# Moving the rounding of finished q and k slabs to the end of their slot in a two-layer hybrid encoder kernel

## The reference

```
h = rmsnorm(x, g_mix[l]);  proj = h @ w_in[l];  q, k, v of groups A, B, C = split(proj)
A: a = softmax(q0 k0' - slope*dist) - lam * softmax(q1 k1' - slope*dist);  o = rmsnorm(a @ v, g_sub) * (1 - lam_init)
B: p = softmax with sink over the window of 128 back;  o = p @ v
C: s = q k' + cum_q - cum_k, causal;  o = softmax(s) @ v
x = x + concat(o_a, o_b, o_c) @ w_out[l]
x = x + square(relu(rmsnorm(x, g_mlp[l]) @ w_up[l])) @ w_down[l]
```

## Time and profile before

| | |
|---|---|
| time, median of 3 runs | 2723.97 us (2723.39 to 2725.60) |
| the profiled execution: time and span | 2725.2 us and 2723.4 us |
| PE busy / weight loads busy | 2586.7 us (95%) / 2121.5 us (78%) |
| DVE, ACT, POOL busy | 1156.1 us, 897.2 us, 214.7 us |
| mean granted PE clock | 0.978 |
| attention stretch of layer 0, about 80 to 607 us | PE busy 476.9 of 527 us |
| MLP of layer 0, 607 to 1372 us | PE busy 762.2 of 765 us |

### The profile page before, as it was taken

One profiled execution on the slowest core, in us unless ns is written; L12 is line 12 of the kernel. 1 busy time (PEld: TensorE's weight loads), 2 busy tenths in 40 slices (PEclk: granted clock), 3 DMA queues, 4 the chain that ended last, 5 costly groups with the idle time before them and its releaser, 6 DMA issues.

```text
span 2723.4 us, 33992 instructions
## 1 busy us (share of the span) xinstructions
PE 2586.7 (95%) x12825; PEld 2121.5 (78%) x12825; DVE 1156.1 (42%) x2309; ACT 897.2 (33%) x1572; POOL 214.7 (8%) x101
## 2 busy tenths in 40 slices
PE   7999999879999999999999999997899999999998
PEld 6778777668788888888878877776788888888886
DVE  5554566644322323223336546665533232232333
ACT  5554444432311202112236444444322021120222
POOL 1111011012000000000211111111110000000011
PEclk9999999989999999999999999998999999999998
DMA  5100010211111111111320000002111111111112
GB/s 170 60 24 24 16 31 25 63 45 39 46 54 46 46 54 44 49 46 54 100 79 24 24 24 24 24 24 68 47 47 46 54 45 48 46 54 46 46 46 77
DMA packets 219021, 131.44 MB, mean 48 GB/s; under 512 B 15222, under 2 KB 214432, under 8 KB 218664
## 3 DMA queue, kind: packets, MB, share of 16 engines
q1 hardware_dynamic: 213208, 114.38, 14.6%
q10 hardware_dynamic: 5712, 15.73, 1.5%
HBM read 117.47 MB, written 12.62 MB: 48 GB/s over the span
## 4 chain that ended last, share of the span: by engine, by line
PE 80%; DVE 7%; ACT 5%; issue 5%; DVEq 1%; DMA 0%; POOL 0%; SPq 0%; ACTq 0%; POOLq 0%
PE ps L1139 70%; PE ps L1271 2%; PE ps L1218 2%; PE ps L1291 2%; ACT probs L638 1%; DVE probs L945 1%; DVE probs L917 1%; ACT pt_hi L656 1%; PE ps L1293 1%; DVEq L924 1%; ACT sink_exp L641 1%; DVE pt_lo L968 1%; ACT o_out L673 0%; DVE wide_lo L963 0%; ACT wide_hi L651 0%
## 5 line engine op out<-in xcount | busy, mean ns | idle before, releaser
L1139 PE MATMUL ps<-wide_hi,w_hi 128*128 128x512 f32 x3016 | 962.1, 400 | 49.3 <-POOL w_lo L510 12.2
L1139 PE MATMUL ps<-wide_lo,w_hi 128*128 128x512 f32 x3016 | 939.8, 393 | 0.0
L1139 PE MATMUL ps<-wide_hi,w_lo 128*128 128x512 f32 x3016 | 937.0, 392 | 0.0
L1139 PEld LDWEIGHTS ps<-wide_hi,w_hi 128*128 128x128 f32 x3016 | 554.7, 190 | 183.8 <-issue 56.7
L1139 PEld LDWEIGHTS ps<-wide_lo,w_hi 128*128 128x128 f32 x3016 | 572.5, 190 | 122.9
L1139 PEld LDWEIGHTS ps<-wide_hi,w_lo 128*128 128x128 f32 x3016 | 571.5, 189 | 122.6
L719 ACT ACTIVATE w_hi<-w_raw 128x1024 fp32r<-128x1024 f32 x112 | 117.8, 1052 | 453.1 <-PE ps L1139 443.6
L638 ACT ACTIVATE probs<-probs,neg_max,slope 128x256 f32<-128x256 f32 (+7 forms) x256 | 202.4, 791 | 178.2 <-DVE neg_max L932 115.2
L723 ACT ACTIVATE ring<-ring 128x1024 f32<-128x1024 f32 x64 | 67.8, 1060 | 487.7 <-DVE ring L1074 487.7
L1094 DVE TENSOR_TENSOR xt<-ps,xt 128x1024 f32 x48 | 58.8, 1224 | 387.3 <-PE ps L1139 387.3
L968 DVE TENSOR_TENSOR pt_lo<-ps,pt_hi 128x512 fp32r<-128x512 f32 (+3 forms) x216 | 126.4, 585 | 221.7 <-ACT pt_hi L656 221.0
(11 more groups left out here) (139 smaller groups left out, 1842.8 us busy)
## 6 DMA issues: line engine op xcount, KB each, us to landing
w_raw<-in_w_up_dram SPq DMA_DIRECT2D x128, 256.0 KB, 3.0
w_raw<-in_w_down_dram SPq DMA_DIRECT2D x128, 256.0 KB, 3.0
w_raw<-in_w_in_dram SPq DMA_DIRECT2D x92, 256.0 KB, 3.3
x_saved<-xt ACTq DMA_DIRECT2D x16, 512.0 KB, 2.6
w_raw<-in_w_out_dram SPq DMA_DIRECT2D x32, 256.0 KB, 3.3
xt<-x_saved SPq DMA_DIRECT2D x16, 512.0 KB, 4.0
o_out<-cum_saved ACTq DMA_DIRECT2D x2, 2048.0 KB, 8.5
out_dram<-rows SPq DMA_DIRECT2D x4, 1024.0 KB, 6.3
```

What stands on the lines that cost most here:

```text
L1139: mm = T.matmul(ps[p][:, bass.ts(t, BANK)], w, h[:, bass.ts(t, BANK)], start=(start and n == 0), stop=(stop and n == 2))
```

## The change

In every slot with an ended q or k slab, `part_high` on ACT is issued behind the exponentials, `finish_o` and `half_high`, just ahead of `split_load`, and `part_low` on DVE is issued behind `half_low`, just ahead of `sum_values`. V slabs keep their place. No instruction is added or removed: 13 `part_high` and 13 `part_low` per layer move.

```diff
@@ ACT @@
                 for s in slots:
-                    if s.ended is not None and s.ended < IN:
+                    if s.turns_v is not None:
                         part_high(s.ended)
...
                     if s.half and not ahead:
                         half_high(s.half)
+                    if s.ended is not None and s.ended < IN and s.turns_v is None:
+                        part_high(s.ended)
                     for n in s.split:
                         split_load(l, n)
@@ DVE @@
                     if s.second:
                         biased_max(t, 1)
-                    if s.ended is not None and s.ended < IN:
+                    if s.turns_v is not None:
                         part_low(s.ended)
...
                     if s.half:
                         half_low(s.half)
+                    if s.ended is not None and s.ended < IN and s.turns_v is None:
+                        part_low(s.ended)
                     if s.summed is not None:
                         sum_values(s.summed)
```

## The result

| | before | after |
|---|---|---|
| median (lowest to highest) of 4 runs each, same chip | 2723.68 us (2720.23 to 2725.60) | 2743.85 us (2741.51 to 2745.51) |
| the profiled execution: time and span | 2725.2 and 2723.4 us | 2743.51 and 2741.2 us |
| mean granted PE clock | 0.978 | 0.975 |

After to before is 1.0081, with a 95% interval of 1.0069 to 1.0093: the change costs some 20 us by the medians, 22 by the ratio. The forecast was 2745, in a range of 2731 to 2756.

The account below looks back on a forecast made before the run. PE, with 80% of the chain, was taken to bound the kernel, losing time only where it waits, in attention mainly for DVE. Terms 9.0 + 7.2 + 3.8 - 0.3 + 1.7 = 21.4 us gave 2745 us, range 2731 to 2756.

Parts of the forecast that it names:

- No gain at the front: All 13 slots: no exponential or `half_high` waits for `part_high`, so clearing the front buys nothing, except at slot 46.
- Pairs B: Slots 4, 8, 12 in both layers: the next `biased_max` starts 1.5 us later, passed on in full; 9.0 us.
- the ring: Slots 4, 8, 12: DVE-ACT loop from one `biased_max` to the next, 5.1 us a step, setting the pace.
- Pairs C: Slots 20, 27, 41: DVE late by 0.4 to 1.2 us, but idle soon after; no cost.
- k slabs of pairs A: Slots 66, 78, 90: POOL is held up and `combine` ends later; 1.2 us each, 7.2 us in all.
- q slabs of pairs A: Slots 63, 75: 0.2 us each; slot 87, `variances` operations behind POOL: 1.5 each; 3.8 us together.
- Slot 46: Layer 0 loses a collision with POOL, 0.9 us earlier; layer 1 is 0.6 later; sum -0.3 us.
- Clock: One more stretch of half PE clock behind lengthened waits; +1.7 us, bounds -3.4 and +7.
- faster: Rival, chance 0.03: only the lost collision at slot 46 and half clock stretches count; 6 us gained, 2718.
- only pairs A pay: Rival, chance 0.20: PE's lead swallows most of the delay in pairs B; 2738 us.
- nothing is measurable: Rival, chance 0.10: parts are needed a pair later and DVE has idle time; 2724 to 2728 us.
- `combine` takes the whole 1.95 us: Rival, chance 0.17: whole delay in the k slots, and clock falling in longer waits adds 5.1 us; 2755 us.

Follow-up runs that it names:

- e2: Kernel before with both parts late only in slots 20, 27, 41 and 46: 2718.9 us, 0.9999.
- e5: Kernel before with only `part_low` late, behind `half_low`, in all 13 slots, `part_high` left in front: 2734.45 us, 1.0052.
- e6: Kernel before with only `part_high` late, behind `half_high`, in all 13 slots, `part_low` at its old place: 2744.13 us, 1.0097.
- e9: Kernel before with `half_high` ahead of the exponentials in pairs B: 2708.37 us, 0.9956.
- e3: Kernel before with both parts late only in slots 63, 75 and 87: 2726.08 us, 1.0023.
- e1: Kernel before with both parts late only in slots 4, 8 and 12: 2729.45 us, 1.0037.
- e8: Kernel before with `split_load` of slots 46, 66, 78 and 90 one slot later: 2713.76 us, 0.9980.

## Why the prediction was right, point by point

**No gain at the front: held.** In slot 4 the exponentials and `pt_hi` start within 0.06 us of where they did.

**Pairs B, 9.0 us: measured 8.9.** The stages are 4.30 and 4.60 us longer. DVE's own starts show the pattern: `biased_max` falls behind by 1.48 us at five of the six slots, by 1.31 at slot 8 of layer 0, and between them it neither loses nor regains over 0.05 us. The mark that I named for it, 4.5 us a layer in PE's waits, was wrong in form. PE's idle time in the two stages grew by only 1.8 and 2.2 us; the rest is 2.5 and 2.4 us more of *busy* PE, at a lower clock. These windows show it, the first of the whole stage of layer 0 and the second from inside it (the number ahead of the DMA share is the granted clock):

```profile
76.69:165.25 88.56, 79.40 (x467) 64.97 (x468) 51.91 (x199) 51.06 (x147) 9.74 (x4) 0.96 0.15 48
...
131.00:138.00 7.00, 7.00 (x32) 5.60 (x32) 2.17 (x12) 4.93 (x18) 0.00 (x0) 0.76 0.12 36
```

In the second PE is busy throughout with the clock at 0.76, and the ring's steps in it are 4.65 and 5.13 us, as they were before at full clock. The extra busy time need not come from the change at all. Stage B of layer 0 is the same code in e2 as in the kernel before, and its profile has a stretch at half clock there that the other has not (first the kernel before, then e2):

```profile
76.75:161.01 84.26, 76.86 (x467) 63.69 (x468) 52.64 (x199) 51.08 (x148) 9.48 (x4) 0.98 0.16 51
...
76.84:161.07 84.23, 77.89 (x467) 64.77 (x468) 52.64 (x199) 51.07 (x148) 9.50 (x4) 0.96 0.16 51
```

PE is busy 1.03 us more and the stage is as long as before. The ring sets the length, and whether PE fills it slowly or waits is the same to the end. e5 and e6 lengthen the ring by other amounts than the change, and the stages follow each time; e9 shortens it, and they get shorter.

**Pairs C, 0: held** (e2; a cost of up to 2.5 us would lie inside its interval).

**k slabs of pairs A, 7.2 us: measured 6.1.** By the starts of PE's matmuls each of the six loses 0.99 to 1.04 us, not 1.2. `combine` ends 0.81 after POOL, as forecast; the mis-sized step is how long POOL is held up. I had 0.25 us, the overlap with `k_lo`. Where `k_lo` had 0.23 us left when POOL started, POOL took 2.47 us against 2.41 otherwise. e5 has longer overlaps, 0.70 us at slot 87 and 1.12 at slot 46 of layer 1:

```profile
466.25 1.22 DVE L845 TENSOR_TENSOR q_lo<-part,q_hi 128x1024 fp32r<-128x1024 f32 x1
...
466.77 2.94 POOL L512 TENSOR_TENSOR w_lo<-w_raw,w_hi 128x1024 fp32r<-128x1024 f32 x1 [20.72 <-ACT w_hi L548]
...
1620.66 1.21 DVE L847 TENSOR_TENSOR k_lo<-part,k_hi 128x1024 fp32r<-128x1024 f32 x1
...
1620.76 3.33 POOL L512 TENSOR_TENSOR w_lo<-w_raw,w_hi 128x1024 fp32r<-128x1024 f32 x1 [16.42 <-ACT w_hi L548]
```

In both, POOL ends 2.2 us after the DVE operation does, and so it does after the overlap of 0.23 (363.08 against 360.84) and of 0.91; undisturbed it lasts 2.4. POOL is blocked in full until some 0.2 us before the recorded end of the DVE operation, an estimate from these rows, and an overlap with this last piece costs next to nothing. The Trainium skill (SBUF — State Buffer, section on who interferes with whom) has the shared ports as an exclusive lock. The rows agree in both directions, up to these 0.2 us; nothing here says where they come from.

**q slabs of pairs A, 3.8 us: measured 3.5.** Slots 63 and 75 lose 0.22, 0.19, 0.21 and 0.22 us (forecast 0.2 each), slot 87 1.34 and 1.35 (forecast 1.5).

**Slot 46, -0.3 us: measured -0.5**, by the waits of the earlier trace rows: 0.9 less in layer 0, 0.4 more in layer 1.

**Clock, +1.7 us: about 0 in the profiled pair.** The terms above make 8.9 + 6.1 + 3.5 - 0.5 = 18.0, and the spans differ by 17.8. Stretches at half clock came and went on both sides, 1.2 to 1.6 us each. Behind slot 46, for instance, there was a long one in layer 0 and a short one in layer 1; in the changed kernel the long one is in layer 1. Layer 0 gains there, layer 1 loses, and neither was foreseen. The medians differ by 20.2 us and the two profiled executions by 18.3, since that of before took 1.5 us more than the median; so two microseconds need not be in the traces at all.

Behind slot 87 the clock does follow the wait. The wait is 0.99 to 1.03 us in the ten profiles that leave this slot's parts in front or move them to the next slot, and in none of their 20 passes (two layers each) does half clock begin within 4 us of its end. It is 1.91 to 2.39 in the changed kernel, e3, e5 and e6, and in 7 of 8 passes half clock begins within 2 us. The stretch behind the wait that ended at 469.34 before and at 474.64 after:

```profile
469.50:474.00 4.50, 4.50 (x31) 3.55 (x32) 3.18 (x13) 2.04 (x3) 0.18 (x1) 1.00 0.35 105
...
475.00:479.50 4.50, 4.50 (x22) 3.78 (x22) 2.02 (x9) 1.08 (x2) 0.00 (x0) 0.62 0.25 75
```

So that a longer wait can bring a stretch, as the forecast had it, has support at this one place, while other stretches went and the sum of them came to nothing. One bound of this term was also added up wrongly. With both stretches behind slot 46 gone it is 3.4 + 1.7 = 5.1 us less, as the rival "faster" has it, and not 3.4; the range would have begun at 2729.

**Luck.** The forecast of 21.4 us lies 1.2 from the difference of the medians, but the terms measured in the traces make 18.0: each was forecast too high, by 0.1, 1.1, 0.3, 0.2 and 1.7 us. That the total fits better than its terms is luck.

**The rivals.** That only pairs A pay is out by e1 (10 us from pairs B alone). That nothing is measurable is out by the result; that the kernel gets faster is out too, although its mechanism was real: the collision in slot 46 did go and brought 0.9 us. That `combine` takes the whole 1.95 us is out by slot 66 (1.0). That clock adds 5 us to the sum isn't seen in the pair of profiles, but single kernels (e3, e5) are some 3 to 6 us above what their rows explain. The stretches behind slot 87 (two in each of these two profiles, 1.2 to 1.6 us each) could be a part of that; it stays open.

## What to carry to other kernels

In these kernels an engine that runs its instructions in order had cover only ahead of a wait: work put there was free up to the length of the wait, and the same work put behind it delayed what followed, although DVE is busy only 42% of the span. Before moving anything, follow the ring across engines from one step to the next; here it ran DVE, ACT, DVE, and one edit that took a link out of it (e9) was worth 12 us, where moving work within it cost 9. And keep an operation of GpSimd that reads SBUF away from VectorE's operations with two SBUF inputs, tiny ones too: four loads a layer split a slot later gave 5.4 us.

## What was not expected of the hardware

An instruction on one column can cost as much as POOL's whole one. In the kernel before, in layer 0 behind slot 8:

```profile
123.75 0.15 DVE L889 TENSOR_TENSOR neg_lam<-lam_dot 128x1 f32<-128x1 f32 x1
123.80 2.37 POOL L510 TENSOR_TENSOR w_lo<-w_raw,w_hi 128x1024 fp32r<-128x1024 f32 x1 [18.04 <-ACT w_hi L546]
...
124.05 2.14 DVE L889 TENSOR_TENSOR neg_lam<-lam_dot 128x1 f32<-128x1 f32 x1
```

The same operation takes 0.15 us just ahead of POOL.

Half clock falls behind some waits and not others of the same length, and behind the same wait in one profile and not in another. In the kernel before it comes after 1.04 us at 1616.32, but not after 1.75 us at 127.46. In e3, whose code is the same in both places, it is the other way round: none after 1.05 us at 1616.32, and one that begins where the wait of 1.75 at 127.33 ends. Only the long waits behind slot 87 brought it nearly always. One stretch more or less (1.2 to 1.6 us) is about what two profiles of nearly equal kernels differ by in a stage.

With the waits out of pairs B (e9) the stage behind them was 2.7 us shorter in each layer. In layer 0 PE is busy for 66.92 us there instead of 68.91, and the granted clock is 1.00 instead of 0.98: two of the 2.7 us are clock given back, one stage later. That the edit gave it back is not shown: in e8, which leaves pairs B alone, the same two stages have no half clock either and are 1.9 and 1.6 us shorter.
